# Four re-orderings in a two-block transformer kernel: weight low parts, bank rings, merge low parts, and the inverse's first tile

## The reference

```python
gates = jax.nn.sigmoid(g + b_gate[l])
merged = (g_a * jnp.einsum("bsk,kd->bsd", o_a, w_branch_a[l])
          + g_b * jnp.einsum("bsk,kd->bsd", o_b, w_branch_b[l]))
mix = jnp.einsum("bsd,de->bse", merged, w_out[l])
x = layer_norm(DEEPNORM_ALPHA * x + mix, ln1_g[l], ln1_b[l])
h = jnp.square(jax.nn.relu(jnp.einsum("bsd,df->bsf", x, w_ff1[l])))
```

## Time and profile before

| | |
|---|---|
| Median of 3 runs | 1535.6 us (1535.31 to 1537.13) |
| The profiled execution, its own time | 1537.3 us |
| Span from its first to its last instruction | 1535.5 us |
| Mean granted TensorE clock | 0.990 |
| Instructions in the span | 18703 |

### The profile page before, as it was taken

How to read it: one execution, slowest core, us unless ns; L and a number is a source line. 1 busy time by engine, 2 the same in 40 slices (tenths; PEclk the granted TensorE clock), 3 DMA queues, 4 the chain that set the end, 5 groups by cost and what they waited for, 6 DMA issues and landing times.

```text
span 1535.5 us, 18703 instructions
## 1 busy us (share of the span) xinstructions
PE 1484.0 (97%) x7256; PEld 1189.2 (77%) x7256; DVE 812.9 (53%) x1421; ACT 626.2 (41%) x1139; POOL 131.6 (9%) x108
## 2 busy tenths in 40 slices
PE   7999999999999999999999999999987999999997
PEld 6777677777778888888868777887775888888886
DVE  4543466545754343434568766445563663564453
ACT  4544355532442232313257653344442441342333
POOL 0000100012100000000220002600020110110012
PEclk9999999999999999999999999999998999999999
DMA  6222122222322223332323221000221323233221
GB/s 241 83 78 95 55 69 69 83 69 69 110 82 97 96 96 96 96 96 96 121 85 110 69 69 56 28 15 15 83 96 55 97 95 110 83 104 102 93 71 57
DMA packets 39687, 130.22 MB, mean 85 GB/s; under 512 B 4656, under 2 KB 5040, under 8 KB 39600
## 3 DMA queue, kind: packets, MB, share of 16 engines
q1 hardware_dynamic: 39600, 129.03, 25.8%
HBM read 124.82 MB, written 4.19 MB: 84 GB/s over the span
## 4 chain that ended last, share of the span: by engine, by line
PE 88%; DVE 5%; ACT 3%; issue 2%; POOL 1%; DMA 1%; SPq 0%; POOLq 0%; DVEq 0%; ACTq 0%
PE bank L1111 84%; PE bank L1114 3%; DVE Fm L1776 2%; ACT Fm L1441 2%; DVE Wlo L1776 1%; ACT Whi L1441 1%; POOL Fm L2318 1%; DVE Fm L1784 1%; DMA Wraw<-in_w_in_dram 0%; DVE Fm L1875 0%; ACT Rm L1441 0%; DMA Fm<-in_relb_dram 0%; DVE Xf L1776 0%; ACT L1441 0%; DVE Rm L1776 0%
## 5 line engine op out<-in xcount | busy, mean ns | idle before, releaser
L1111 PE MATMUL bank<-Rm,Whi 128*128 128x512 f32 x2816 | 875.0, 392 | 0.0
L1111 PEld LDWEIGHTS bank<-Rm,Whi 128*128 128x128 f32 x2816 | 532.9, 189 | 108.4 <-issue 0.7
L1111 PE MATMUL bank<-Rm,Wlo 128*128 128x512 f32 x1408 | 567.0, 403 | 30.2 <-issue 10.4
L1111 PEld LDWEIGHTS bank<-Rm,Wlo 128*128 128x128 f32 x1408 | 266.4, 189 | 93.3 <-issue 32.4
L1776 DVE TENSOR_TENSOR Wlo<-Wraw,Whi 128x1024 fp32r<-128x1024 f32 (+1 forms) x224 | 275.5, 1234 | 86.5 <-ACT Whi L1441 86.4
L1441 ACT ACTIVATE Whi<-Wraw 128x1024 fp32r<-128x1024 f32 (+1 forms) x224 | 232.6, 1042 | 214.6 <-PE bank L1111 206.8
L1111 PE MATMUL bank<-Xr,Whi 128*128 128x512 f32 x736 | 226.8, 389 | 0.0
L2318 POOL TENSOR_TENSOR Fm<-Fm 128x512 f32<-128x512 f32 x94 | 126.1, 1351 | 969.3 <-DVE Fm L1784 444.0
L1441 ACT ACTIVATE Fm<-bank 128x512 f32<-128x512 f32 (+4 forms) x227 | 97.7, 459 | 186.7 <-PE bank L1111 121.0
L1111 PEld LDWEIGHTS bank<-Xr,Whi 128*128 128x128 f32 x736 | 138.5, 188 | 28.8
L1776 DVE TENSOR_TENSOR Fm<-Fm,bank 128x512 f32<-128x512 f32 (+1 forms) x138 | 79.0, 602 | 143.8 <-PE bank L1111 143.8
(11 more groups left out here) (95 smaller groups left out, 798.7 us busy)
## 6 DMA issues: line engine op xcount, KB each, us to landing
Wraw<-in_w_in_dram SPq DMA_DIRECT2D x68, 512.0 KB, 3.5
Wraw<-in_w_ff_dram SPq DMA_DIRECT2D x64, 512.0 KB, 3.5
Wraw<-in_w_up_dram SPq DMA_DIRECT2D x44, 512.0 KB, 3.5
Wraw<-in_w_o_dram SPq DMA_DIRECT2D x16, 512.0 KB, 3.5
Wraw<-in_w_down_dram SPq DMA_DIRECT2D x16, 512.0 KB, 3.5
Wraw<-in_w_ab_dram SPq DMA_DIRECT2D x8, 512.0 KB, 3.5
Wraw<-in_w_down_end_dram SPq DMA_DIRECT2D x8, 384.0 KB, 2.9
Fm<-in_x_dram SPq DMA_DIRECT2D x8, 256.0 KB, 6.8
```

The source lines that it names most:

```text
L1111: return e.matmul(o, l, r, start=first, stop=last)
```

## The change

There are four edits and the code they need.

1. In `project_first`, `ready_weights` now comes before `low_weights`, so the low part of the fifth panel is issued on DVE right after the three panels, ahead of their evictions.
2. The ring of the panels begins elsewhere: (1, 2, 4, 0) for `w_ab`, (2, 3, 1, 0) for `w_o_2`.
3. The low part of merged tile j-1 becomes an item of its own (`mergelow`), issued after `merge` j.
4. `first` disappears as an item of DVE; POOL makes that tile inside `lower`, between its two levels. `decay0` of the four heads moves to the ends of the projections t = 10, 11, 16, 17. The decays take 8 steps instead of 9, placed 2, 3, 3 in the three panels.

```diff
--- before.py
+++ after.py
@@ -136,7 +136,7 @@
 
 STEPS_A, STEPS_B, STEPS_GATE = 1, 2, 2
 STEPS_UNIT = (2, 1, 1, 2, 1, 1)
-STEPS_DECAYS = (3, 3, 3)
+STEPS_DECAYS = (2, 3, 3)
 STEPS_INVERSE = (9, 8)
 STEPS_SCAN = (8, 8)
 
@@ -222,8 +222,8 @@
                 for item in between[step]:
                     do(*item)
         st["done"] = ns[-1] + 1
+        ready_weights(st["taken"] + 2)
         low_weights()
-        ready_weights(st["taken"] + 2)
         return ns
 
     do("ring", "P", (0, 1))
@@ -340,7 +340,7 @@
     run(side, 999)
 
 
-    do("ring", "P", (0, 1, 2, 4))
+    do("ring", "P", (1, 2, 4, 0))
     do("ring", "S", (3,))
     do("ring", "T", (5,))
     for i in (0, 2, 3, 4, 5, 6, 7):
@@ -356,6 +356,9 @@
         low_weights()
         for j in range(i, i + len(ns)):
             do("merge", j)
+            if j > 0:
+                do("mergelow", j - 1)
+    do("mergelow", 7)
 
     def residual(name, tag, sums):
         first = project_first([(name, i) for i in range(BEGUN)])
@@ -474,6 +477,8 @@
             do("gates2", t - 1)
         if t in (7, 8):
             do("gates2", t - 2)
+        if t in (10, 11, 16, 17):
+            do("decay0", (10, 11, 16, 17).index(t))
         if t == 5:
             do("factors", 0)
         if 6 <= t <= 9:
@@ -489,8 +494,8 @@
 
 
     def gdn_decays():
-        for i in range(9):
-            for kind, h in (("decay0", i), ("decay1", i - 1), ("decay2", i - 2), ("lower", i - 3), ("first", i - 4), ("inv0", i - 5)):
+        for i in range(8):
+            for kind, h in (("decay1", i), ("decay2", i - 1), ("lower", i - 2), ("inv0", i - 4)):
                 if 0 <= h < 4:
                     do(kind, h)
             yield
@@ -563,7 +568,7 @@
     run(side, 99)
 
 
-    do("ring", "P", (0, 1, 2, 3))
+    do("ring", "P", (2, 3, 1, 0))
     do("reload")
     do("rmsg")
     for h in range(4):
@@ -631,7 +636,7 @@
         ("scan1", 0): (), "scan1": ("wks",), "scan2": ("kus", "os"),
     },
     "v_delta": {
-        "decay0": ("gt",), "decay2": ("decayed",), "lower": ("lt", "attn", "qd"), "first": ("xt_first",),
+        "decay0": ("gt",), "decay2": ("decayed",), "lower": ("lt", "attn", "qd"),
         "invb": ("xt",), "solve": ("gkt",), "ke": ("ke",), "scan1": ("u",),
         "scan2": ("state",),
     },
@@ -908,7 +913,7 @@
                     return (SG["head_hi"], at("headout", k)), (SG["head_lo"], at("headout", k))
                 return (SG["feat_hi"], at("feat", k)), (SG["feat_lo"], at("feat", k))
             if name == "w_o":
-                return (SG["merged_hi"], at("merge", k)), (SG["merged_lo"], at("merge", k))
+                return (SG["merged_hi"], at("merge", k)), (SG["merged_lo"], at("mergelow", k))
             if name == "w_ff1":
                 return (SG["y_hi"], at("splity", k)), (SG["y_lo"], at("splity", k))
             if name == "w_ff2":
@@ -1343,7 +1348,7 @@
 
                 elif what == "inv0":
                     h, = i
-                    w.wait_ge(*sig("xt_first", "first", h))
+                    w.wait_ge(SG["xt_first"], at("lower", h))
                     bank_free("inv0", h)
                     for _, s in tiles4():
                         m = tr(bank("inv0", h)[:, s], G(3 * h + 1)[:, s])
@@ -1947,8 +1952,11 @@
                     tt(ga, ga, b, ALU.mult).then_inc(SG["merge_a"], 1)
                     w.wait_ge(SG["gated1"], 8 + j + 1)
                     tt(gb, gb, bank("panelb", n), ALU.mult).then_inc(SG["merge_b"], 1)
+
+                elif what == "mergelow":
+                    j, = i
                     w.wait_ge(SG["merged_hi"], at("merge", j))
-                    tt(R(2 * j + 1), ga, R(2 * j).bitcast(F32), ALU.subtract).then_inc(SG["merged_lo"], 1)
+                    tt(R(2 * j + 1), F(GATE_HOMES[j]), R(2 * j).bitcast(F32), ALU.subtract).then_inc(SG["merged_lo"], 1)
 
                 elif what == "mixed":
                     n, = i
@@ -2173,12 +2181,6 @@
                     w.wait_ge(*sig("eg", "decay2", h))
                     tt(F(GQ + h), F(GQ + h), F(EG + h), ALU.mult).then_inc(SG["v_delta"], 1)
 
-                elif what == "first":
-                    h, = i
-                    w.wait_ge(*level_made(h, 0))
-                    tt(by_tile(G(3 * h + 1)), every_tile(ident), by_tile(F(level_home(h, 0))),
-                       ALU.subtract).then_inc(SG["v_delta"], 1)
-
                 elif what == "invb":
                     h, n = i
                     w.wait_ge(*sig("invb", "invb", h, n))
@@ -2362,13 +2364,15 @@
                     w.wait_ge(*sig("lt", "lower", h))
                     w.wait_ge(*sig("attn", "lower", h))
                     level(h, 0)
+                    w.wait_ge(*level_made(h, 0))
+                    tt(by_tile(G(3 * h + 1)), every_tile(ident), by_tile(F(level_home(h, 0))), ALU.subtract).then_inc(SG["xt_first"], 1)
                     w.wait_ge(*sig("qd", "lower", h))
                     level(h, 1)
 
                 elif what == "inva" and i[1] < 5:
                     h, n = i
                     if n == 1:
-                        w.wait_ge(*sig("xt_first", "first", h))
+                        w.wait_ge(SG["xt_first"], at("lower", h))
                     else:
                         w.wait_ge(*sig("inva", "inva", h, n - 1))
                     level(h, n + 1)
```

## The result

The changed kernel took 1521.54 us (median of 4 runs, 1518.81 to 1525.28), the kernel before, measured beside it, 1536.37 (1535.31 to 1540.2): a ratio of 0.9901, 95% interval 0.9873 to 0.9929. The forecast was 1515.3 with a range of 1510.5 to 1523: faster, as predicted, but 6 us short of the number. The profiled execution has a span of 1520.6 us and its own time is 1522.41, against 1535.5 and 1537.3: 14.9 us gained where the sum said 20.25. The measured median lies outside the forecast's own bounds (1510.5 to 1519) and inside the range because the range was drawn out to the rivals.

A forecast was written before the change was run, and what follows sets the result against it. PE, busy 97% of the span, was taken as the bound: its work plus waits and low-clock stretches. Gains A 5.95, B 3.9, C 4.5, D 5.2, F 1.2, less E 0.5, sum to 20.25: 1515.3 us against the median, range 1510.5 to 1523.

The forecast's parts named there:

- A: `w_ab` stage: new ring and later merge low part gain 5.95 us together, 2.85 + 1.7 + 1.4.
- third term: In A: `merge` 1 is freed, the chain is 1.4 us earlier, and the 2.38 wait before `w_o` becomes 1.0.
- F: Decays and inverse: DVE loses eight products, POOL makes the first tile; gain 1.2 us, between 2.4 gained and 1.7 lost.
- first two terms: In A: the wait before panel 40 goes, 2.85 us, and the low clock following it goes, 1.7.
- Rival 1: The clock is not won back because short waits left in A and C bring it again: 1520.3 us; chance 0.11.
- B: `w_ff1` start: panel 60's low part is ready earlier; gain 2.18 for the wait plus 1.7 for the clock, 3.9 us.
- D: `w_up` start: panel 160's low part comes earlier, the wait of 10.37 becomes 4.9; gain 5.2 us.
- C: `w_o_2` start: wait of 3.85 and low clock (1.65) go, two new waits of 0.5 come; gain 4.5 us.
- E: `w_in_2` start: `betas` wait for DVE's low part of `wba`, now behind panel 124's; loss 0.5 us, between 0 and 1.2.
- Rival 3: The ring does not free A because another thing is late at 311.6; 4.55 us stays, 1519.9; chance 0.06.
- rival 4: Slower: evictions or low parts behind the split hold PE as long, so B, C, D bring nothing: 1540 us; chance 0.04.

The follow-up runs named there:

- x2: Kernel before with only the two rings of panels changed, (1, 2, 4, 0) and (2, 3, 1, 0): 1533.35 us, ratio 0.9977.
- y1: Changed kernel, but only tile 0's merge low part comes a tile later, the others right after their own tile: 1517.57 us, ratio 0.987 to the kernel before.
- x3: Kernel before with only the merge low part of tile j-1 moved behind `merge` j: 1540.69 us, ratio 1.0013.
- x1: Kernel before with only `ready_weights` put ahead of `low_weights` in `project_first`: 1526.73 us, ratio 0.9934.
- y2: Changed kernel with the low parts of panels 161 and 162 issued ahead of `w_up`'s first gated tile on DVE: 1514.02 us, ratio 0.9859 to the kernel before.
- y4: Changed kernel, but POOL makes level 1 of head 2 after head 3's first tile instead of before it: 1518.39 us, one run.
- y5: Changed kernel with panel 50, the third of `w_o`, in bank 3 instead of the bank of panel 47: 1520.36 us, ratio 0.9892 to the kernel before.
- y7: Changed kernel with the inverse's first tile given back to DVE, the decays staying where the change put them: 1520.17 us, one run.
- z: Changed kernel with y6's loop, y2, y4, and panel 124's low parts back behind `betas`: 1517.08 us, ratio 0.9859 to the kernel before.
- x4: Kernel before with only the decays earlier and the first tile of the inverse on POOL: 1536.59 us, ratio 1.0001.
- y6: Changed kernel with the `w_ab` loop turned: merge first, then its low part, then the weights' low parts: 1525.09 us, ratio 0.9915 to the kernel before.

## Why the prediction was right in its sign and off in its size

**A failed in its third term.** "The merge low part lies beside the split, so moving it does not shorten the period" is true and was not the question: moved, it lies beside POOL's add, and lengthens it. GpSimd's timeline after, with the merge low part of VectorE beside it:

```profile
354.16 0.69 DVE L1781 TENSOR_TENSOR Rm<-Fm,Rm 128x512 fp32r<-128x512 f32 x1
...
354.39 1.60 POOL L2320 TENSOR_TENSOR Fm<-Fm 128x512 f32<-128x512 f32 x1 [4.21 <-DVE Fm L1781]
```

The add starts inside the DVE product and takes 1.60; before it took 1.29, as it does in x2 and y1. The merges then start (352.97 - 341.33)/2 = 5.82 us apart instead of 5.50:

```profile
322.73 1.28 DVE L1781 TENSOR_TENSOR Fm<-Fm,bank 128x512 f32<-128x512 f32 x2 [1.36 <-PE bank L1116]
...
341.33 1.28 DVE L1781 TENSOR_TENSOR Fm<-Fm,bank 128x512 f32<-128x512 f32 x2
...
352.97 1.28 DVE L1781 TENSOR_TENSOR Fm<-Fm,bank 128x512 f32<-128x512 f32 x2
...
358.78 1.28 DVE L1781 TENSOR_TENSOR Fm<-Fm,bank 128x512 f32<-128x512 f32 x2
```

The first of these rows is `merge` 1, which now waits for PE and is no longer late; the last is `merge` 7. From one to the other it is 36.05 us, before 362.72 - 328.57 = 34.15. These 1.9 us, 0.32 for each of six steps, eat the 1.4 that tile 0 gave and 0.5 more, by which the wait before `w_o` grew. Part A had 1.4 of gain and a wait of 1.0 there; measured is a loss of 0.53 and a wait of 2.91.

The Trainium skill, "SBUF — State Buffer", section "Who interferes with whom", states that a VectorE instruction with two SBUF inputs contends with a GpSimd instruction that reads SBUF, and that the pair of ports they share is an exclusive lock. The trace agrees (1.60 for 1.29, with x3 and y1 as its test). The prediction's "for the whole instruction" that section says only of VectorE's modes with two ports; here a product of 0.69 that overlaps the add by at most 0.46 costs it 0.31. The prediction had weighed the same rule in F and not asked it in A. Its first two terms held: PE runs dry at 359.60 - 2.91 = 356.69, before at 361.16, and the last tiles ahead of the stage start 0.21 later (311.18 for 310.97), so 4.68 was won against 2.85 + 1.7 = 4.55. Then 0.53 goes to the longer wait and about 1.6 to the clock of 0.60 (4 us) behind it. Rival 1 was right that a wait left in A can bring the low clock again, and wrong about the three places that it priced, where the clock is 1.00; its 1520.3 lies near the measured time for another reason, so that is luck.

**B, D and F were right in size**: 4.02 for 3.9, 5.08 for 5.2, 1.32 for 1.2. F's wait is ended by POOL as forecast; GpSimd's timeline has two levels, made beside DVE's low part, at 4.00 for 2 x 1.28:

```profile
954.45 4.00 POOL L2320 TENSOR_TENSOR Fm<-Fm 128x512 f32<-128x512 f32 x2
958.53 1.26 POOL L2320 TENSOR_TENSOR Xf<-CC,Fm 128x512 f32<-128x512 f32 x1
```

**C** gave 4.14 for 4.5, with 0.44 and 0.49 for its two estimates of 0.5. **E** cost 0.45 for 0.5, with a wait of 0.55. Rival 3 and rival 4 fell, since no wait stands at 311.6 and none of 2 us before panels 61, 153 or 158.

**Not in the sum** were 1.61 us in the scan. Windows of the 14.5 us behind the same PE wait, first the changed kernel, then the one before:

```profile
1025.50:1040.00 14.50, 14.31 (x76) 10.23 (x76) 7.78 (x34) 5.93 (x24) 0.00 (x0) 0.76 0.00 1
```

```profile
1032.80:1047.30 14.50, 14.36 (x84) 9.80 (x85) 8.46 (x37) 7.56 (x33) 0.00 (x0) 0.88 0.00 1
```

The wait ahead of them is 0.82 in both. At 0.76 for 0.88 the same stretch loses 14.5 x 0.12 = 1.7. The prediction had no term for the clock here. Of the runs here x1, x2, x3, y2, y4, y5, y7 and z have 1.00 from 1020 to 1040, y1 and the kernel before 0.91, and x4, y6 and the change, in both of its profiles, 0.83. What decides it is open. Each is one execution, the change two. A's 3.6 and this 1.6 make 5.2 of the 5.4 us between 20.25 and 14.86; the other parts together fell 0.2 short.

## What to carry to other kernels

An instruction moved out of a chain lands beside something: ask what runs there, and what the two cost each other side by side, before it is costed at nothing. In a chain over several engines whose period is near the bound engine's pace, 0.3 us a step is paid at the end as many times as there are steps (six here, 1.9 us). And where PE waits for the first of several small products in one queue, order them by when PE needs them: that was 10 us here and 5 more in `w_up`, while before `w_o` another bank (y5) or a turned loop (y6) only changed the name of what was late.

## What the runs showed of the hardware that was not expected

- The clock behind a wait is not set by that wait alone. Windows of 4 us from PE's restart at `w_o`, x1 and x2, each after a wait of 2.38:

```profile
363.70:367.70 4.00, 3.98 (x18) 3.33 (x19) 1.61 (x3) 1.58 (x2) 1.29 (x1) 1.00 0.43 131
```

```profile
361.20:365.20 4.00, 3.97 (x11) 3.18 (x12) 1.62 (x3) 1.58 (x2) 1.28 (x1) 0.61 0.47 135
```

  In four traces with the wait of 2.87 some 50 us earlier (before, x1, x3, x4, with waits of 2.38, 2.38, 2.91 and 2.38 at `w_o`) the clock stays at 1.00. In those without it, it falls behind waits of 2.38 (x2) and of 2.9 or 3.99 (the change, y2, y4, y6, y7, z), and not behind 1.32 and 2.31 (y1, y5). The wait of 2.87 itself is followed by 0.57 to 0.61 over 4 us in before, x1 and x3, and by 1.00 in x4, where the same instructions run up to there; and one wait of 2.19 before the inverse is followed by 1.00 in the kernel before and by 0.60 in x2. First x4 behind 2.87, then the kernel before and x2 behind 2.19:

```profile
315.44:319.44 4.00, 4.00 (x18) 3.31 (x19) 1.54 (x2) 0.81 (x1) 0.00 (x0) 1.00 0.28 72
```

```profile
957.45:961.45 4.00, 3.44 (x19) 2.69 (x20) 4.00 (x12) 1.61 (x3) 4.00 (x3) 1.00 0.00 0
```

```profile
955.05:959.05 4.00, 4.00 (x13) 3.34 (x14) 4.00 (x12) 1.55 (x2) 4.00 (x3) 0.60 0.00 0
```

  These are single executions, and the ten runs of the changed kernel have mean granted clocks from 0.991 to 0.998, so the clock also differs between executions of one kernel. A wait taken away can give back a part of its worth at the next one: in x2 PE restarts at `w_o` 2.31 us earlier than before, 4.66 if one takes off that its whole trace lies 2.35 later up to the last gate panel (303.13 for 300.78), and the low clock there takes 4 x 0.39 = 1.6 of it. Why it falls is open.
- A POOL add held by one DVE product loses less than the product's length where they overlap in part: 1.60 for 1.29 beside a product of 0.69 that had begun 0.23 us before, 0.3 us for an overlap of at most 0.46.
